# w_up: two of the three split products as one matmul of 512 columns, in a fp32 decoder trunk on one core

## What is computed

```python
h = rms_norm(x, norm_ffn_g[i])
u = causal_dwconv(h @ w_up[i], ffn_conv_w[i])
u_g, u_v = jnp.split(u, 2, axis=-1)
x = x + (jax.nn.silu(u_g) * u_v) @ w_down[i]
```

## Time and profile before

| | us |
|---|---|
| median of 3 runs | 1643.11 (1642.69 to 1646.19) |
| profiled execution, its time | 1643.69 |
| its span, first to last instruction | 1641.6 |
| PE busy in it | 1625.0 |
| DVE busy | 1004.2 |
| ACT busy | 753.9 |
| granted TensorE clock, mean | 0.998 of full |

### The profile page before, as it was taken

One profiled execution on the slowest core, in us unless ns is written; L12 is line 12 of the kernel. 1 busy time (PEld: TensorE's weight loads), 2 busy tenths in 40 slices (PEclk: granted clock), 3 DMA queues, 4 the chain that ended last, 5 costly groups with the idle time before them and its releaser, 6 DMA issues.

```text
span 1641.6 us, 28848 instructions
## 1 busy us (share of the span) xinstructions
PE 1625.0 (99%) x11554; PEld 1533.2 (93%) x11554; DVE 1004.2 (61%) x1181; ACT 753.9 (46%) x913; POOL 32.3 (2%) x53
## 2 busy tenths in 40 slices
PE   7999999999999999999999999999999999999998
PEld 7989998999999999988899999988899999988887
DVE  6599655664566545555466677665446666764554
ACT  5444443434555444545444444443334454454443
POOL 5000000000000000000000000000000000000000
PEclk9999999999999999999999999999999999999999
DMA  7666555555555555555565665566565656556564
GB/s 237 181 180 177 168 147 153 166 165 157 175 166 164 173 186 183 183 190 183 168 178 179 192 180 178 178 200 195 192 186 165 190 180 194 183 178 197 179 201 146
DMA packets 154277, 294.34 MB, mean 179 GB/s; under 512 B 9383, under 2 KB 11795, under 8 KB 154192
## 3 DMA queue, kind: packets, MB, share of 16 engines
q1 hardware_dynamic: 153648, 292.85, 57.6%
q0 software_dynamic: 512, 0.27, 0.1%
q10 hardware_dynamic: 32, 0.01, 0.0%
HBM read 291.00 MB, written 2.10 MB: 179 GB/s over the span
## 4 chain that ended last, share of the span: by engine, by line
PE 98%; DVE 1%; DMA 0%; ACT 0%; issue 0%; POOL 0%; SPq 0%; ACTq 0%; DVEq 0%
PE acc L450 22%; PE acc L451 22%; PE acc L452 22%; PE acc L475 10%; PE acc L477 10%; PE acc L476 10%; PE fb L555 1%; DMA xtok<-in_x 0%; PE fa L492 0%; PE fa L509 0%; PE fb L600 0%; PE fa L600 0%; PE fa L569 0%; PE fb L588 0%; PE fb L578 0%; ACT junk L801 0%
## 5 line engine op out<-in xcount | busy, mean ns | idle before, releaser
L1057 DVE TENSOR_TENSOR w_lo<-raw,w_hi 128x1024 fp32r<-128x1024 f32 x550 | 670.4, 1224 | 584.1 <-ACT w_hi L784 583.8
L784 ACT CAST w_hi<-raw 128x1024 fp32r<-128x1024 f32 x550 | 571.6, 1048 | 668.2 <-PE acc L452 440.4
L450 PE MATMUL acc<-h_hi,w_hi 128*128 128x256 f32 x2704 | 769.4, 285 | 3.0 <-DVE h_lo L1063 3.0
L452 PE MATMUL acc<-h_hi,w_lo 128*128 128x256 f32 x2704 | 765.9, 283 | 0.0
L451 PE MATMUL acc<-h_lo,w_hi 128*128 128x256 f32 x2704 | 765.9, 283 | 0.0
L450 PEld LDWEIGHTS acc<-h_hi,w_hi 128*128 128x128 f32 x2704 | 519.7, 192 | 3.7 <-issue 3.2
L451 PEld LDWEIGHTS acc<-h_lo,w_hi 128*128 128x128 f32 x2704 | 519.7, 192 | 0.1
L452 PEld LDWEIGHTS acc<-h_hi,w_lo 128*128 128x128 f32 x2704 | 519.5, 192 | 0.0
L475 PE MATMUL acc<-w_hi,f_hi 128*128 128x512 f32 x352 | 137.3, 390 | 0.0
L476 PE MATMUL acc<-w_lo,f_hi 128*128 128x512 f32 x352 | 137.0, 389 | 0.0
L477 PE MATMUL acc<-w_hi,f_lo 128*128 128x512 f32 x352 | 137.0, 389 | 0.0
(11 more groups left out here) (252 smaller groups left out, 1240.0 us busy)
## 6 DMA issues: line engine op xcount, KB each, us to landing
raw<-in_w_up SPq DMA_DIRECT2D x176, 512.0 KB, 3.6
raw<-in_w_gate SPq DMA_DIRECT2D x96, 512.0 KB, 3.8
raw<-in_w_in SPq DMA_DIRECT2D x90, 512.0 KB, 3.6
raw<-in_w_down SPq DMA_DIRECT2D x88, 512.0 KB, 4.3
raw<-in_w_out SPq DMA_DIRECT2D x32, 512.0 KB, 3.7
raw<-in_w_ple_gate SPq DMA_DIRECT2D x32, 512.0 KB, 4.3
raw<-in_w_moba_out SPq DMA_DIRECT2D x16, 512.0 KB, 3.7
raw<-in_w_conv_out SPq DMA_DIRECT2D x8, 512.0 KB, 3.7
```

Of the source, the lines that this page charges most:

```text
L450: nc.tensor.matmul(dst, stat_hi, mov_hi, start=first, stop=False, skip_group_check=True)
L452: return nc.tensor.matmul(dst, stat_lo, mov_hi, start=False, stop=last, skip_group_check=True)
L784: A.copy(w_hi[:, c % RING, :], raw[:, c % RING, :]).then_inc(chunk_high, 1)
L1057: V.tensor_tensor(w_lo[:, c % RING, :], raw[:, c % RING, :], w_hi[:, c % RING, :].bitcast(F32), ALU.subtract).then_inc(chunk_split, 1)
```

## The change

In both up stages a chunk's products are grouped otherwise. h_hi and h_lo now lie side by side in one tile `h_both`, 256 high columns and 256 low ones for each of 16 row blocks. For each of the chunk's eight weight blocks one matmul of 512 columns holds w_hi and moves both; it writes a whole bank, high x high in the first half, high x low in the second. Eight narrow matmuls with w_lo and h_hi follow, which add to the second half. A part now fills four banks (`wide[0]` = banks 0 to 3, `wide[1]` = banks 4 to 7), which `acc`, `fa` and `fb` share. The two halves must be added: ACT copies the second into upg or upv, DVE adds the first (which frees the banks), and then scales by rB. The spread of rB goes to `fb` instead of `fa`, and PE waits for its copy (`rB_taken`) before the first part 1. All other stages keep their matmuls.

```diff
-    h_hi = new("h_hi", [P, KD, S], F32R)
-    h_lo = new("h_lo", [P, KD, S], F32R)
+    h_both = new("h_both", [P, KD, 2, S], F32R)
+    h_hi, h_lo = h_both[:, :, 0, :], h_both[:, :, 1, :]
...
+    psum = nc.alloc_psum_tensor("psum", [P, 8, 512], F32)
+    acc = [psum[:, b:b + 2, :].rearrange("p b (j s) -> p (b j) s", j=2) for b in (0, 6)]
+    fa = psum[:, 2:4, :]
+    fb = psum[:, 4:6, :]
+    wide = [psum[:, QD * i:QD * i + QD, :] for i in range(2)]
...
+        def wide_chunk(c, part, kt, first, last, i, step):
+
+            pe.wait_ge(chunk_split, i * step + (c + 1))
+            tiles = [(k, j, slice(k * W + j * P, k * W + (j + 1) * P)) for k in range(2) for j in range(QD)]
+            for k, j, w in tiles:
+                nc.tensor.matmul(wide[part][:, j, :], w_hi[:, c % RING, w], h_both[:, kt + k, :, :].rearrange("p h s -> p (h s)"),
+                                 start=first and k == 0, stop=False, skip_group_check=True)
+            for k, j, w in tiles:
+                mm = nc.tensor.matmul(wide[part][:, j, S:2 * S], w_lo[:, c % RING, w], h_hi[:, kt + k, :],
+                                      start=False, stop=last and k == 1, skip_group_check=True)
+            mm.then_inc(chunk_used, 1)
...
-        spread(8, fa_flat, 1)
+        spread(8, fb_flat, 1)
...
                     pe.wait_ge(taken[part], i + group0 // 2)
+                    if part == 1 and u_first:
+                        pe.wait_ge(rB_taken, 1)
...
-                        feature_chunk(c0 + 8 * part + j, part, h_hi, h_lo, 2 * j, j == 0, j == 7, i, 16)
+                        wide_chunk(c0 + 8 * part + j, part, 2 * j, j == 0, j == 7, i, 16)
...
+        def low_part(k, dst, i, used):
+
+            act.wait_ge(chunk_used, used)
+            earlier()
+            A.copy(dst[:, :, 2:], wide[k][:, :, S:2 * S]).then_inc(low_sums, 1)
+
+        def taps0(src, dst, col, i, need):
+
+            act.wait_ge(up_scaled, need)
...
-                taps0(1, upv, cv, FT + 4 * pair0, i, i + (group0 // 2 + 1))
-                for k in range(20, 23):
+                low_part(1, upv, i, i * 16 + (c0 + 16))
+                high(c0 + 20, i, 16)
+                taps0(upv, cv, FT + 4 * pair0, i, i * 2 + (2 * pair0 + 2))
+                for k in range(21, 23):
...
+                def scaled(k, dst, i, count, groups):
+
+                    dve.wait_ge(low_sums, count)
+                    V.tensor_tensor(dst[:, :, 2:], wide[k][:, :, 0:S], dst[:, :, 2:], ALU.add).then_inc(taken[k], 1)
+                    dve.wait_ge(taken[k], groups)
+                    V.tensor_tensor(dst[:, :, 2:], dst[:, :, 2:], quad(rB[:]), ALU.mult).then_inc(up_scaled, 1)
...
-                dve.wait_ge(chunk_used, i * 16 + (c0 + 16))
-                V.tensor_tensor(upv[:, :, 2:], acc[1][:], quad(rB[:]), ALU.mult).then_inc(taken[1], 1)
+                scaled(1, upv, i, i * 2 + (2 * pair0 + 2), i + (group0 // 2 + 1))
```

More of the change, by code:

```diff
@@ L221, in trunk @@
     fin = ar("fin", [P, 2, TT, W], 36.5)
-    acc = [nc.alloc_psum_tensor(f"acc{i}", [P, QD, S], F32) for i in range(2)]
-    fa = nc.alloc_psum_tensor("fa", [P, 2, 512], F32)
-    fb = nc.alloc_psum_tensor("fb", [P, 2, 512], F32)
+    psum = nc.alloc_psum_tensor("psum", [P, 8, 512], F32)
[3 more added lines that the diff above has]
+    wide = [psum[:, QD * i:QD * i + QD, :] for i in range(2)]
     def flat(t):
@@ L266, in trunk @@
     cv_ready = sem("cv_ready")
+    rB_taken, low_sums, up_scaled = sem("rB_taken"), sem("low_sums"), sem("up_scaled")
     def unit_dst(u):
@@ L961, in _ @@
                     x_high(g, g, R_FFN)
-        def taps0(k, src, dst, col, i, need):
-            act.wait_ge(taken[k], need)
+        def low_part(k, dst, i, used):
[4 more added lines that the diff above has]
+            act.wait_ge(up_scaled, need)
             earlier()
@@ L973, in up @@
                 highs[0] = i * 16 + (c0 + 12)
-                taps0(0, upg, cg, 4 * pair0, i, i + (group0 // 2 + 1))
-                for k in range(12, 15):
+                low_part(0, upg, i, i * 16 + (c0 + 8))
+                high(c0 + 12, i, 16)
+                taps0(upg, cg, 4 * pair0, i, i * 2 + (2 * pair0 + 1))
+                for k in range(13, 15):
                     high(c0 + k, i, 16)
@@ L1391, in _ @@
                 dve.wait_ge(rs_spread, 6)
-                step(V.tensor_copy(rB[:], fa[:, 0, 0:S]))
+                V.tensor_copy(rB[:], fb[:, 0, 0:S]).then_inc(rB_taken, 1)
+                dve.wait_ge(rB_taken, 1)
                 V.memset(upg[:, :, 0:2], 0.0)
@@ L1397, in _, with up @@
         d0 = steps[0]
-        def up(c0, pairs, pair0, u0, d0):
+        def up(c0, pairs, group0, pair0, u0, d0):
             with dve.Fori(0, pairs) as i:
+                def scaled(k, dst, i, count, groups):
[3 more added lines that the diff above has]
+                    V.tensor_tensor(dst[:, :, 2:], dst[:, :, 2:], quad(rB[:]), ALU.mult).then_inc(up_scaled, 1)
                 def conv(src, dst, col, taps):
@@ L1420, in up @@
                 dve.wait_ge(chunk_split, i * 16 + (c0 + 12))
-                dve.wait_ge(chunk_used, i * 16 + (c0 + 8))
-                V.tensor_tensor(upg[:, :, 2:], acc[0][:], quad(rB[:]), ALU.mult).then_inc(taken[0], 1)
+                scaled(0, upg, i, i * 2 + (2 * pair0 + 1), i + (group0 // 2 + 1))
                 split(c0 + 12, i, 16)
@@ L1453, in up @@
             return d0 + 2 * pairs
-        d0 = up(UP1, PAIRS1, 0, U_F, d0)
+        d0 = up(UP1, PAIRS1, NG_UP1, 0, U_F, d0)
         n = K1 // 2
@@ L1465, in _ @@
                         V.tensor_tensor(v, v, tokens(acc[half]), ALU.add).then_inc(taken[half], 1)
-        d0 = up(UP2, PAIRS2, PAIRS1, U_F + PAIRS1, d0)
+        d0 = up(UP2, PAIRS2, NG_UP2, PAIRS1, U_F + PAIRS1, d0)
         steps[0] = d0
```

## The result

| | before, us | changed, us |
|---|---|---|
| median | 1643.22 | 1627.98 |
| executions | 1642.69 to 1646.19 (4) | 1627.26 to 1630.09 (4) |
| profiled execution's span | 1641.6 | 1625.3 |

The ratio is 0.9906, with a 95% interval of 0.9889 to 0.9923: faster by 0.9%. Forecast were 1627.8 us and a range of 1623 to 1631.

A forecast was written before the change was run, and what follows sets the result against it. PE was taken as the bound, never waiting in the up stages. 8 x 0.0133 - 0.02 = 0.087 us a chunk over 176 chunks gave -15.3 from 1643.69, so 1628.4, median 1627.8 us; range 1623.0 to 1631.0.

The forecast's parts named there:

- The price of a fused pair: PE, up stages: joining two narrow matmuls into one wide saves 0.0133 us, 18.8 us over 176 chunks.
- The changes of width: PE, up stages: going narrow to wide and back costs net 0.02 us a chunk, 3.5 us given back.
- rival A: PE, up stages: the changes of width cost nothing, so -18.8 us, 1624.3 us; chance 0.22.
- The sum: Up stages: 0.087 us saved a chunk over 176 chunks, -15.3 us, median 1627.8 us.
- The cover: Up stages, part 1: chunk 23's split ends at 17.2 us, PE wants it at 19.56, 2.3 us to spare.
- Rival C: Up stages: longer chain holds chunk 23's split beyond PE's need; 0.5 us beyond the spare costs 5.5; partly 0.05, slower 0.02.
- Rival B: PE, up stages: a wide matmul holding w_hi costs two narrow ones, 0.2400 us, so no change, 1643.1 us; chance 0.04.
- Rival D: PE, up stages: another bank at every matmul costs; at 10 ns each, 1656 us; partly 0.04, slower 0.03.
- DMA, rB_taken, the moved spread: DMA at 188 GB/s in up stages, and the one-time wait and spread for rB, cost nothing.

The follow-up runs named there:

- experiment 2: Changed kernel with its eight weight blocks reordered so that two matmuls in a row write the same bank: 1628.44 us.
- experiment 4: Changed kernel with the order of wide and narrow turned round in every second chunk, so half the width changes go: 1626.94 us, repeated 1626.60.
- experiment 1: Changed kernel with only the fusing undone, each wide matmul split into two of 256 columns: 1643.74 us against 1643.38, ratio 0.9999.
- experiment 3: Changed kernel with wide and narrow matmuls in turn, one of each per weight block: median 1633.62 us, repeated 1634.28.
- experiment 5: Changed kernel with wide and narrow matmuls in runs of four: 1630.22 us; in runs of two: 1628.58 us.
- experiment 6: Changed kernel with unread 128x1024 DVE operations added in part 1 before the scaling: two more 1630.68 us, four more 1655.55 us.

## Why the prediction was right

- **The price of a fused pair** (0.0133 us, from one pitch for each shape): right. The sixth to eighth wide starts are 227 ns, the later narrow ones 120.
- **The changes of width** (0.02 us a chunk): right, 0.020 (2.793 us against the 2.773 of steady starts). I could not tell whether it hangs on the width or on weights and activations changing sides; here they keep their sides, and the sizes are the same, so it is the width (experiments 2 and 4 take out bank and chunk border, experiment 1 the step from w_hi to w_lo). Why a change of width costs that is not shown, and experiments 3 and 5 show that the price by position holds only for long runs, as here. Without this term, as in rival A, I would have said 1624.3, 3.7 us too low.
- **The sum**: 15.3 us foreseen in the profiled span's up stages, 15.2 measured. The span itself fell by 16.3; 0.9 of the other 1.1 lies ahead of the first up stage, which now begins at 798.15 instead of 799.06, and is the clock's and not the change's: executions differ in where the granted clock falls to half, 1.2 GHz for 2.4. The profile before has such a stretch about 265 us in, and the one after has none there and a longer one in its first 40 us (granted clock 0.91 there, 0.96 before). By the starts of the same matmuls on PE, the changed kernel is 0.71 us behind the kernel before from 26 to 206 us, and 0.91 ahead from 278 us on. The medians fell by 15.2. That the forecast lies within 0.2 us of the median is in part luck, as single executions differ by up to 3 us. Five microseconds of that stretch, before and then after (the clock is the third number from the end):

```profile
265.00:270.00 5.00, 5.00 (x16) 3.96 (x15) 0.99 (x2) 0.86 (x1) 0.60 (x1) 0.66 0.32 101
```

```profile
265.00:270.00 5.00, 5.00 (x23) 4.12 (x23) 2.06 (x3) 1.05 (x1) 1.30 (x1) 1.00 0.43 134
```

- **The cover**: split of chunk 23 foreseen at 17.2 us with 2.3 to spare, measured 17.35 with 2.2; experiment 6 found the edge there. Rival C's price of lateness was right but for 0.10 us more at each wait; the second place, chunk 21, is reached only with a shift of 4.0 us.
- **Rivals B and D** fell with the wide pitch of 0.2267 and with experiments 1 and 2. The Trainium skill ("TensorE: Matmul & The Clock Gate", "Back-to-back issue gap") gives 2.5 ns beyond the columns, for a gap that it calls isolated. The rows of both kernels have 13.3, with a weight load for each matmul. An estimate by the Trainium skill's 2.5 ns: the fused pairs would have saved 3.5 us, and the changes of width would have taken as much back.
- **DMA, rB_taken, the moved spread**: nothing was foreseen. PE has no idle time in the up stages, and 188 GB/s flowed.

## What to carry to other kernels

Where PE never idles, read the distance between starts for each shape in its own stretch: two widths give the fixed part of a matmul, and with it what joining two is worth. Then read the transitions too, since an order that switches between shapes pays them every time; keep runs of one shape long (turn the order round in every second block). A price read behind long runs held for runs of eight and 16 here, but not for runs of one and two, and for runs of four only in the sum: measure such orders. A drain that becomes longer costs nothing as long as the first late operand has time to spare; find which one that is by walking the chain once, and prove it by adding work until PE waits.

## What the runs showed that I had not expected

- A stream of alternating 512 and 256 column matmuls runs at 2.774 or at 2.827 us a chunk of 16, constant through a stage, with the same instructions and a full clock.
- In runs of eight and 16 each shape has one rate from the sixth wide and the third narrow start on, but the first five wide starts behind a narrow run are 7, 9, 2, 6 and 4 ns longer, 27 in sum before rounding, and only 7.5 of these come back on the way to narrow.
- Shorter runs follow other patterns: with runs of two a chunk takes 2.787 us, less than with runs of eight (2.793), though it has four times as many changes of width.
- The first matmul of a chunk for which PE had to wait starts its successor 0.10 us late, on top of the wait (experiment 6).
